# The norms of three seven-product stages: sums by a one-column matrix, rstd to rows by way of DRAM

## The chip, the cores and the metric

The kernel runs on one core of one Trainium2 chip. The metric is the device time of one execution in microseconds (us), as the median of several runs.

## The reference

One inference step of a decoder trunk of two layers, for 1,024 prompt tokens and 64 sample tokens that share their weights (1,088 tokens, model width 1,024). Layer 0 mixes tokens by sparse attention, layer 1 by a chunked gating unit; a SwiGLU follows each.

```python
def rms_norm(x, g):
    xf = x.astype(jnp.float32)
    y = xf * lax.rsqrt(jnp.mean(xf * xf, axis=-1, keepdims=True) + EPS)
    return (y * g.astype(jnp.float32)).astype(x.dtype)

def swiglu(h, w_gu, w_down):
    gate, up = jnp.split(h @ w_gu, 2, axis=-1)
    return (jax.nn.silu(gate) * up) @ w_down

# for each layer i
        xp = xp + mp          # mixer(rms_norm(x)): attention, or the gating unit (h @ w_in, gelu, ...)
        xs = xs + ms
        xp = xp + swiglu(rms_norm(xp, norm_ffn[i]), ffn_w_gu[i], ffn_w_down[i])
        xs = xs + swiglu(rms_norm(xs, norm_ffn[i]), ffn_w_gu[i], ffn_w_down[i])
```

The change concerns three of the norms: those ahead of the two SwiGLUs and the one ahead of the gating unit.

## The kernel before

Activations lie in SBUF with features on the 128 partitions and the 1,088 tokens along a row (`xT`, eight tiles). Each float32 operand is split in a high and a low part (ScalarE writes the high part, `high...`; VectorE subtracts for the low part, `low`, `w_low`), and TensorE multiplies high by high, high by low and low by high.

The three stages of the change are `ffn_stage`, run twice (`ffn0`, `ffn1`), and `gate_stage` (`sgin`). Each multiplies the activations by weights in sets, and each set is made of seven block products (a Strassen scheme with `PRODUCTS = 7`), named p = 0 to 6 here: `B11, T1, T2, B21, T3, B22, T4`. A product is 24 matmuls with 272 columns into one of four pairs of PSUM banks. `ffn_stage` has 22 sets, `gate_stage` eight. The weights of set n + 1 are summed, split and made ready by VectorE and ScalarE while TensorE works on set n, and so are the results of set n combined: `make_u2`, `make_u4`, `make_g0` (the gate's left half, times `rows`), `make_c22` and so on. Product 6 of a set writes the banks that `make_c22` reads, so it waits for it: `FREE_NOW = {3: t_ready, 5: u2_ready, 6: c22_ready}`.

The gain of the norm is put on the activations ahead of the products; the factor 1/rms of each token (`rstd`) is put on the results afterwards, by a multiplication with `rows`, a [128, 1088] tile that holds the token's rstd on every partition. It is made during set 0, in this order: ScalarE squares the last tile into `rows`, VectorE adds the squares of the others; TensorE sums over partitions with the squares as the stationary operand (`column_sums_wide`, bank 6) between products 1 and 2; VectorE and ScalarE make rstd from the sums, which are a [128, 9] tile (`Rstd`: mean, square root, reciprocal and a Newton step); TensorE spreads rstd to all partitions by nine matmuls against the identity (`SPREAD`), between products 2 and 3; ScalarE copies the result to `rows`.

The order of every engine's work is written out by hand; nothing is scheduled by a planner. Waits are on semaphores. SyncE issues nearly all DMAs; a set's weights are loaded (`load_set`) once the low parts of the set before are written. The attention part has a `search_stage` with norms of its own, which are made in the other way: a matrix with one column of ones (`pick`) is stationary, the squares move, the sums land as 8 rows of 136 tokens (`PairRstd`), and rstd goes through DRAM (`r_kept`) to rows.

## Time and profile before

| | |
|---|---|
| median of 3 runs | 2520.27 us (2519.26 to 2523.59) |
| the profiled execution's own time | 2533.14 us |
| its span in the trace | 2531.4 us |
| TensorE (PE) busy | 2444.0 us, 97% of the span |
| VectorE (DVE) busy | 1827.9 us, 72% |
| ScalarE (ACT) busy | 1130.0 us, 45% |
| GpSimd (POOL) busy | 108.3 us, 4% |
| mean granted TensorE clock | 0.987 of full speed |

The profiled execution is one of its own and took 0.5% longer than the median; its trace is read for durations and waits. Busy shares are means over stages that differ. The `ffn0` stage begins at 778 us of the span, `sgin` at 1488 us, `ffn1` at 1804 us; set 0 takes the first 26 us or so of each.

### The profile page before, as it was taken

To read this page: it belongs to the slowest core of one execution; us is meant where nothing else is said; L and a number is where in the kernel's file an instruction comes from. 1 tells how busy PE (TensorE), PEld (TensorE's weight loads), DVE (VectorE), ACT (ScalarE), POOL (GpSimd) and SP (SyncE) were. 2 spreads that over 40 slices of the span, in tenths; PEclk is the share of its full clock that TensorE was granted. 3 is DMA by queue.
4 is the path that set the end of the run, shared out by engine and by line. 5 is a ranking of instruction groups with operands and counts; after the bars stand their busy time and mean duration, and the time that the engine had idled before them with its cause. 6 is when DMAs were issued, how large, how long until landed. Compare 5 with 4: busy or idle time off the path is not lost. (4 is left out here: it accounts for less than half of the span.)

```text
span 2531.4 us, 49311 instructions
## 1 busy us (share of the span) xinstructions
PE 2444.0 (97%) x18922; PEld 2332.5 (92%) x18953; DVE 1827.9 (72%) x3377; ACT 1130.0 (45%) x1928; POOL 108.3 (4%) x140
## 2 busy tenths in 40 slices
PE   8999898899999999999999999989999999999998
PEld 7899865577899999999999999989999999999998
DVE  6668867777558888886685686764798888768642
ACT  5567677686534433333222353553443434322221
POOL 1310132200000000000000000000000000000000
PEclk9899999999999999999999999999999999999999
DMA  6312499820022343433694423234143434449522
GB/s 213 88 51 80 145 332 361 329 84 1 21 100 70 139 147 138 147 138 124 241 321 150 134 73 113 68 94 168 56 139 138 148 138 151 140 177 351 193 91 84
DMA packets 279016, 371.91 MB, mean 147 GB/s; under 512 B 20747, under 2 KB 219651, under 8 KB 270662
## 3 DMA queue, kind: packets, MB, share of 16 engines
q1 hardware_dynamic: 266998, 294.23, 34.3%
q0 software_dynamic: 11776, 75.50, 8.1%
q8 instruction: 101, 1.65, 0.3%
q14 instruction: 61, 0.50, 0.1%
q10 hardware_dynamic: 80, 0.02, 0.0%
HBM read 271.07 MB, written 98.63 MB: 146 GB/s over the span
## 5 line engine op out<-in xcount | busy, mean ns | idle before, releaser
L1554 PE MATMUL ffn_acc<-trunk_x_ahead,trunk_w_hi 128*128 128x272 f32 x2464 | 466.5, 289 | 2.7 <-PEq L87 2.7
L1554 PE MATMUL ffn_acc<-ffn_x_later,ffn_w_hi_more 128*128 128x272 f32 x2112 | 397.1, 287 | 1.5 <-DVE trunk_xT L1203 1.4
L1554 PEld LDWEIGHTS ffn_acc<-trunk_x_ahead,trunk_w_hi 128*128 128x128 f32 x2464 | 385.3, 188 | 3.3 <-issue 3.3
L1554 PE MATMUL ffn_acc<-trunk_x_ahead,trunk_w_lo 128*128 128x272 f32 x1232 | 352.9, 286 | 0.0
L1554 PEld LDWEIGHTS ffn_acc<-ffn_x_later,ffn_w_hi_more 128*128 128x128 f32 x2112 | 330.9, 188 | 2.3 <-issue 2.3
L1554 PE MATMUL ffn_acc<-ffn_x_later,ffn_w_lo_more 128*128 128x272 f32 x1056 | 304.1, 288 | 0.0
L1554 PEld LDWEIGHTS ffn_acc<-trunk_x_ahead,trunk_w_lo 128*128 128x128 f32 x1232 | 232.5, 189 | 0.0
L1554 PEld LDWEIGHTS ffn_acc<-ffn_x_later,ffn_w_lo_more 128*128 128x128 f32 x1056 | 198.8, 188 | 0.0
L1445 DVE TENSOR_TENSOR trunk_xT<-ffn_acc,trunk_xT 128x544 f32<-128x544 f32 x168 | 121.4, 723 | 92.9 <-PE ffn_acc L1610 91.0
L1610 PE MATMUL ffn_acc<-trunk_x_ahead,trunk_w_hi 128*128 128x272 f32 x896 | 170.8, 289 | 0.0
L945 ACT ACTIVATE ffn_w_hi_more<-trunk_w_raw 128x512 fp32r<-128x512 f32 x132 | 83.3, 631 | 156.2 <-PE ffn_acc L1554 153.5
L945 ACT ACTIVATE trunk_w_hi<-ffn_w_sum 128x512 fp32r<-128x512 f32 x88 | 55.6, 632 | 210.2 <-DVE ffn_w_sum L1184 125.4
L1610 PE MATMUL ffn_acc<-ffn_x_later,ffn_w_hi_more 128*128 128x272 f32 x768 | 145.8, 287 | 0.1
L1634 PE MATMUL ffn_acc<-trunk_x_ahead,trunk_w_hi 128*128 128x364 f32 (+1 forms) x576 | 142.1, 328 | 0.0
L1610 PEld LDWEIGHTS ffn_acc<-trunk_x_ahead,trunk_w_hi 128*128 128x128 f32 x896 | 140.1, 188 | 0.4 <-issue 0.4
L1610 PE MATMUL ffn_acc<-trunk_x_ahead,trunk_w_lo 128*128 128x272 f32 x448 | 128.3, 286 | 0.0
L3321 PE MATMUL search_acc<-attxm_x_pairs,attxm_w_hi 128*128 128x364 f32 (+1 forms) x480 | 121.4, 334 | 1.9 <-PEq L87 1.9
L1610 PEld LDWEIGHTS ffn_acc<-ffn_x_later,ffn_w_hi_more 128*128 128x128 f32 x768 | 120.2, 188 | 0.7 <-issue 0.3
L1032 ACT ACTIVATE trunk_xT<-trunk_xT 128x544 fp32r<-128x544 f32 x112 | 71.7, 654 | 91.5 <-DVE trunk_xT L1264 48.8
L1610 PE MATMUL ffn_acc<-ffn_x_later,ffn_w_lo_more 128*128 128x272 f32 x384 | 110.5, 288 | 0.0
L1203 DVE TENSOR_TENSOR trunk_xT<-ffn_acc,ffn_u 128x544 f32<-128x544 f32 x88 | 63.5, 722 | 59.2 <-PE ffn_acc L1554 59.2
L1634 PEld LDWEIGHTS ffn_acc<-trunk_x_ahead,trunk_w_hi 128*128 128x128 f32 x576 | 101.8, 188 | 0.0
(523 smaller groups left out, 5994.6 us busy)
## 6 DMA issues: line engine op xcount, KB each, us to landing
o_kept<-trunk_xT SPq DMA_DIRECT2D x96, 544.0 KB, 4.4
trunk_w_raw<-in_ffn_w_gu SPq DMA_DIRECT2D x88, 512.0 KB, 4.0
trunk_x_ahead<-o_kept SPq DMA_DIRECT2D x56, 544.0 KB, 6.7
ffn_x_later<-o_kept SPq DMA_DIRECT2D x56, 544.0 KB, 7.3
x_saved<-trunk_xT SPq DMA_DIRECT2D x24, 544.0 KB, 2.7
trunk_xT<-x_saved SPq DMA_DIRECT2D x24, 544.0 KB, 6.6
o_kept<-trunk_xT SPq DMA_DIRECT2D x32, 272.0 KB, 4.9
trunk_w_raw<-in_sg_w_in SPq DMA_DIRECT2D x16, 512.0 KB, 4.0
```

The lines of the kernel that those rows point to most:

```text
L945: nc.scalar.activation(w_parts(i)[0], source, ACT.Copy).then_inc(w_hi_ready, 1)
L1032: nc.scalar.activation(stage_hi[STAGE_OF[i][0]], raw_block[i], ACT.Copy).then_inc(kept_hi, 1)
L1203: nc.vector.tensor_tensor(two(out), pair(b), two(a), ALU.add).then_inc(done, 1)
L1445: nc.vector.tensor_tensor(two(out), pair(bank_of(z, n)), two(out), ALU.add).then_inc(d_added, 1)
L1554: last = nc.tensor.matmul(bank(2 * PAIR[p] + c)[:, 0:QC], w[:, k * P:(k + 1) * P], x(p, k)[:, c * QC:(c + 1) * QC], start=FRESH[p] and k = ...
L1610: last = nc.tensor.matmul(bank(2 * bank_of(z, n) + c)[:, 0:QC], w[:, k * P:(k + 1) * P], x(i, at)[:, c * QC:(c + 1) * QC], start=n in (0, ...
L1634: last = nc.tensor.matmul(bank(NC3 * (q % 2) + c)[:, 0:w], part[:, q % 2, k * P:(k + 1) * P], x[:, a:a + w], start=(k == 0 and j == 0), st ...
L3321: last = nc.tensor.matmul(banks[NC3 * (m % 2) + c][:, 0:w], part[:, k * P:(k + 1) * P], x_parts[x][:, k, a:a + w], start=(k == 0 and j == ...
```

## The change

Three things are done in `ffn_stage` and `gate_stage`. The sums over partitions are made as in `search_stage`: a [128, 32] window on a matrix with one column of ones is stationary and 136 tokens of squares move, in eight matmuls that fill four groups of 32 PSUM partitions (`row_sums`). rstd is then made on [128, 136] tiles (those of `Rstd` lie in `g0`, in the gate stage in `v_sq`). The nine spreading matmuls and ScalarE's three copies are gone; ScalarE issues four DMAs that store rstd's rows to DRAM (`s_kept`) and, four activations later, one that loads it to all 128 partitions of `rows`. On VectorE, `make_g0(0)` moves from the middle of the `low(T4, ...)` steps to behind `sum_1(1)`, and in the gate stage `make_c11(0)` and `norm_c22(0)` move there too. `pick` becomes one tile for the whole trunk, filled in the first stage.

```diff
-def column_sums_wide(nc, out, squares, ones):
-    for t in range(NTT):
-        a = min(t * P, TOK - P)
-        last = nc.tensor.matmul(out[:, t:t + SUM_W], squares[:, a:a + P], ones[:, 0:SUM_W], start=True, stop=True)
+def row_sums(nc, out, squares, pick):
+    for f in range(2):
+        for c in range(4):
+            a = (2 * c + f) * PIECE
+            last = nc.tensor.matmul(out[32 * c:32 * c + 32, 0:PIECE], pick[:, 3 - f:35 - f], squares[:, a:a + PIECE],
+                                    start=f == 0, stop=f == 1, skip_group_check=True)
     return last
...
-        R = Rstd(S, bank(6)[:, 0:NTT], NTT, D)
+        R = Rstd(S, bank(6)[:, 0:PIECE], PIECE, D, tiles=g0)
...
-            for i, (t0, t1, b, at) in enumerate(SPREAD):
-                act.wait_ge(spread, i + 1)
-                x0, x1 = t0 * P, min(t1 * P, TOK)
-                nc.scalar.activation(rows[:, x0:x1], bank(b)[:, at:at + x1 - x0], ACT.Copy).then_inc(rows_ready, 1)
+            act.wait_ge(R.link, R.READY)
+            for c in range(4):
+                act.dma_start(s_kept[c], R.r[32 * c:32 * c + 2, :]).then_inc(rows_kept, 16)
             for k in range(KH):
                 high(B22, k)
+            act.wait_ge(rows_kept, 64)
+            act.dma_start(rows[:, :], s_kept.rearrange("c f n -> (c f n)").unsqueeze(0).to_broadcast([P, TOK])).then_inc(rows_ready, 16)
             for k in range(KH):
                 high(T4, k)
...
             make_u2(0)
-            dve.wait_ge(rows_ready, 3)
             make_u4(0)
             for k in range(KH):
                 low(B22, k)
-            low(T4, 0)
-            low(T4, 1)
-            make_g0(0)
-            low(T4, 2)
-            low(T4, 3)
+            for k in range(KH):
+                low(T4, k)
             make_c22(0)
             low_1(1)
             sum_1(1)
+            dve.wait_ge(rows_ready, 16)
+            make_g0(0)
             w_low(1, 2, A_S1, E[:, :])
...
-            column_sums_wide(nc, bank(6), rows, g["ones"]).then_inc(summed, 1)
+            row_sums(nc, bank(6), rows, g["pick"]).then_inc(summed, 1)
             product(0, 2, True)
-            pe.wait_ge(R.link, R.READY)
-            for t0, t1, b, at in SPREAD:
-                for tt in range(t0, t1):
-                    skip = tt * P - min(tt * P, TOK - P)
-                    last = nc.tensor.matmul(bank(b)[:, at + (tt - t0) * P:at + (tt - t0 + 1) * P - skip],
-                                            R.r[:, tt:tt + 1].to_broadcast([P, P]), g["ident"][:, skip:P],
-                                            start=True, stop=True)
-                last.then_inc(spread, 1)
             product(0, 3, True)
-            pe.wait_ge(rows_ready, 3)
+            pe.wait_ge(R.link, 1)
             for p in range(4, PRODUCTS):
                 product(0, p, True)
```

The same edits are made in `gate_stage`, where `norm_c22(0)` follows `make_c11(0)` behind `sum_1(1)`. In the first stage GpSimd sets `pick` to zero and writes its column; in `search_stage` it no longer does.

VectorE in set 0 of `ffn0`, from the low parts of `B22` and `T4` to the first low part of set 1's weights; `ffn_x_later` are the low parts of activations, `trunk_xT<-ffn_acc,ffn_u` is `make_c22`, `ffn_gate` is `g0`. Before:

```order
L1151 TENSOR_TENSOR ffn_x_later<-trunk_xT,ffn_x_later 128x544 x6
L1215 TENSOR_TENSOR ffn_gate_10897<-ffn_acc,ffn_rows 128x544
L1151 TENSOR_TENSOR ffn_x_later<-trunk_xT,ffn_x_later 128x544 x2
L1203 TENSOR_TENSOR trunk_xT<-ffn_acc,ffn_u_10898 128x544
L1176 TENSOR_TENSOR trunk_w_lo<-trunk_w_raw,trunk_w_hi 128x1024
L1184 TENSOR_TENSOR ffn_w_sum<-trunk_w_raw 128x512
L1172 TENSOR_TENSOR trunk_w_lo<-ffn_w_sum,trunk_w_hi 128x512
```

And of the change, the same place:

```order
L1156 TENSOR_TENSOR ffn_x_later<-trunk_xT,ffn_x_later 128x544 x8
L1208 TENSOR_TENSOR trunk_xT<-ffn_acc,ffn_u_10891 128x544
L1181 TENSOR_TENSOR trunk_w_lo<-trunk_w_raw,trunk_w_hi 128x1024
L1189 TENSOR_TENSOR ffn_w_sum<-trunk_w_raw 128x512
L1220 TENSOR_TENSOR ffn_gate_10890<-ffn_acc,ffn_rows 128x544
L1177 TENSOR_TENSOR trunk_w_lo<-ffn_w_sum,trunk_w_hi 128x512
```

The multiplication by `rows` now stands behind `make_c22`, `low_1(1)` and `sum_1(1)`.

ScalarE at the same time: `L1010` are the copies to `rows`, `L939` the high parts of `B22` and `T4`. Before:

```order
L945 ACTIVATE ffn_w_hi_more<-trunk_w_raw 128x512
L939 ACTIVATE ffn_x_later<-trunk_xT 128x544
L1010 ACTIVATE ffn_rows<-ffn_acc 128x512 x2
L1010 ACTIVATE ffn_rows<-ffn_acc 128x64
L939 ACTIVATE ffn_x_later<-trunk_xT 128x544 x8
L956 ACTIVATE trunk_w_hi<-trunk_w_raw 128x1024
```

And of the change:

```order
L949 ACTIVATE ffn_w_hi_more<-trunk_w_raw 128x512
L943 ACTIVATE ffn_x_later<-trunk_xT 128x544
L1013 DMA s_kept<-ffn_gate_10890 2x136 x4
L943 ACTIVATE ffn_x_later<-trunk_xT 128x544 x4
L1017 DMA ffn_rows<-s_kept 128x1088
L943 ACTIVATE ffn_x_later<-trunk_xT 128x544 x4
L960 ACTIVATE trunk_w_hi<-trunk_w_raw 128x1024
```

Three copies have given way to five DMA issues, the last between the high parts of `B22` and those of `T4`.

VectorE at the end of set 0 in `gate_stage`; `trunk_xT<-sgin_acc,sgin_t_u` is `make_c22`, `trunk_xT<-sgin_acc,sgin_rows` is `make_c11`, `trunk_xT<-trunk_xT,sgin_rows` is `norm_c22`. Before:

```order
L2180 TENSOR_TENSOR trunk_xT<-sgin_acc,sgin_rows 128x544
L2102 TENSOR_TENSOR trunk_x_low<-trunk_xT,trunk_x_low 128x544 x2
L2185 TENSOR_TENSOR trunk_xT<-sgin_acc,sgin_t_u_16348 128x544
L2164 TENSOR_TENSOR trunk_xT<-trunk_xT,sgin_rows 128x544
L2127 TENSOR_TENSOR trunk_w_lo<-trunk_w_raw,trunk_w_hi 128x1024
L2135 TENSOR_TENSOR sgin_w_sum<-trunk_w_raw 128x512
L2123 TENSOR_TENSOR trunk_w_lo<-sgin_w_sum,trunk_w_hi 128x512
```

And of the change:

```order
L2101 TENSOR_TENSOR trunk_x_low<-trunk_xT,trunk_x_low 128x544 x2
L2184 TENSOR_TENSOR trunk_xT<-sgin_acc,sgin_t_u_16331 128x544
L2126 TENSOR_TENSOR trunk_w_lo<-trunk_w_raw,trunk_w_hi 128x1024
L2134 TENSOR_TENSOR sgin_w_sum<-trunk_w_raw 128x512
L2179 TENSOR_TENSOR trunk_xT<-sgin_acc,sgin_rows 128x544
L2163 TENSOR_TENSOR trunk_xT<-trunk_xT,sgin_rows 128x544
L2122 TENSOR_TENSOR trunk_w_lo<-sgin_w_sum,trunk_w_hi 128x512
```

Both multiplications by `rows` now come after `sum_1(1)`, in the order `make_c11`, `norm_c22`.

## Rows read from the trace of the kernel before

**Rows 1.** PE timeline, set 2 of ffn0 and sgin: start, length, ..., [idle, releaser]

```profile
844.42 0.49 PE L1554 MATMUL ffn_acc<-ffn_x_later,ffn_w_hi_more 128*128 128x272 f32 x2 [0.69 <-DVE trunk_xT L1203]
...
1554.45 0.48 PE L2373 MATMUL sgin_acc<-sgin_x_high,sgin_w_hi_more 128*128 128x272 f32 x2 [1.25 <-DVE trunk_xT L2185]
```

**Rows 2.** PE timeline of set 0 in ffn0

```profile
785.22 2.14 PE L191 MATMUL ffn_acc<-trunk_ones,ffn_rows 128*128 128x96 f32 x18
...
790.24 2.12 PE L1569 MATMUL ffn_acc<-trunk_ident,ffn_rstd 128*128 128x128 f32 x18
...
801.46 0.50 PE L1554 MATMUL ffn_acc<-ffn_x_later,ffn_w_hi_more 128*128 128x272 f32 x2
```

**Rows 3.** DVE timeline of set 0 in ffn0

```profile
787.48 0.17 DVE L162 TENSOR_SCALAR ffn_mean<-ffn_acc 128x9 f32<-128x9 f32 x1
...
788.19 0.21 DVE L166 RECIPROCAL ffn_rinv<-ffn_root 128x9 f32<-128x9 f32 x1
...
789.13 0.69 DVE L1172 TENSOR_TENSOR ffn_w_lo_more<-trunk_w_raw,ffn_w_hi_more 128x512 fp32r<-128x512 f32 x1
...
798.74 0.72 DVE L1215 TENSOR_TENSOR ffn_gate<-ffn_acc,ffn_rows 128x544 f32<-128x544 f32 x1
799.38 1.35 DVE L1151 TENSOR_TENSOR ffn_x_later<-trunk_xT,ffn_x_later 128x544 fp32r<-128x544 f32 x2
800.64 0.71 DVE L1203 TENSOR_TENSOR trunk_xT<-ffn_acc,ffn_u 128x544 f32<-128x544 f32 x1
...
802.41 0.68 DVE L1184 TENSOR_TENSOR ffn_w_sum<-trunk_w_raw 128x512 f32<-128x512 f32 x1
803.79 0.69 DVE L1172 TENSOR_TENSOR trunk_w_lo<-ffn_w_sum,trunk_w_hi 128x512 fp32r<-128x512 f32 x1 [0.70 <-ACT trunk_w_hi L945]
```

**Rows 4.** busy time by window, from 788 to 801 us

```profile
788.00:801.00 13.00, 13.00 (x109) 13.00 (x108) 12.77 (x25) 9.76 (x18) 0.00 (x0) 1.00 0.30 82
```

**Rows 5.** ACT timeline of set 0 in ffn0

```profile
791.54 1.39 ACT L1010 ACTIVATE ffn_rows<-ffn_acc 128x512 f32<-128x512 f32 x3
792.82 4.49 ACT L939 ACTIVATE ffn_x_later<-trunk_xT 128x544 fp32r<-128x544 f32 x8
```

**Rows 6.** PE timeline of the search stage, one head's sums

```profile
197.07 0.67 PE L3275 MATMUL search_small<-att_proj,search_pick 128*32 128x136 f32 x16
```

**Rows 7.** DVE timeline of the search stage, mean and rstd of a pair

```profile
185.02 0.30 DVE L3127 TENSOR_SCALAR search_head_mean<-search_small 128x136 f32<-128x136 f32 x1
...
189.71 0.99 DVE L3137 RECIPROCAL search_head_rinv<-search_head_root 128x136 f32<-128x136 f32 x1
...
191.88 0.15 DVE L2529 TENSOR_TENSOR search_late_over<-search_late_count,search_late_limit 128x2 f32<-128x2 f32 x1
```

**Rows 8.** SP queue of the search stage, and landing times of its row loads

```profile
192.00 1.32 SPq L3216 DMA_DIRECT2D r_kept<-search_head_rstd  x4
194.23 0.94 SPq L3222 DMA_DIRECT2D search_row_buf<-r_kept  x2
...
DMA to landing us min/median/max: 4.0/4.6/5.5
```

**Rows 9.** DVE and PE timeline of set 0 in sgin

```profile
1509.19 0.72 DVE L2185 TENSOR_TENSOR trunk_xT<-sgin_acc,sgin_t_u 128x544 f32<-128x544 f32 x1
...
1510.59 1.22 DVE L2127 TENSOR_TENSOR trunk_w_lo<-trunk_w_raw,trunk_w_hi 128x1024 fp32r<-128x1024 f32 x1
...
1510.88 0.41 PE L2373 MATMUL sgin_acc<-sgin_x_high,sgin_w_hi_more 128*128 128x272 f32 x2
```

**Rows 10.** DMA issues by size, KB each, median us to landing

```profile
trunk_xT<-x_kept SPq DMA_DIRECT2D x8, 544.0 KB, 9.0
```

**Rows 11.** busy time and granted clock (PEclk) by window: one long idle, one short

```profile
17.70:21.60 3.90, 0.06 (x2) 0.02 (x1) 2.38 (x4) 3.13 (x5) 0.12 (x1) 0.79 0.10 1
21.60:26.60 5.00, 5.00 (x17) 3.85 (x18) 5.00 (x5) 5.00 (x5) 0.00 (x0) 0.50 0.22 2
53.50:58.50 5.00, 3.23 (x20) 3.22 (x20) 4.23 (x8) 3.60 (x8) 0.00 (x0) 1.00 0.00 1
```

More of the change, by code:

```diff
@@ L138, with __init__ @@
 class Rstd:
-    def __init__(self, S, sums, columns, width, name="", like=None, out=None):
+    def __init__(self, S, sums, columns, width, name="", like=None, out=None, tiles=None):
         self.sums, self.width = sums, width
-        if like is None:
+        if tiles is not None:
+            self.mean, self.root, self.y, self.a = (tiles[:, columns * i:columns * (i + 1)] for i in range(4))
+            self.r = self.root
+        elif like is None:
             self.mean, self.root, self.y, self.a, self.r = (S.sb(name + n, [P, columns]) for n in
```

83 lines of the change are left out of this document (34 added, 49 removed).

## The prediction

> **What bounds the kernel now.** I read the page first: TensorE is busy for 97% of the span, so work taken from it looks like time won. But that share is an average, and the change acts in the first 26 us of three stages, so I read next who is waited for there. In set 2 of `ffn0` TensorE stands still for 0.69 us, and in set 2 of `sgin` for 1.25 us, each time for `make_c22`, which frees the banks of product 6 [rows 1]; `ffn1` has the same wait as `ffn0`. The timeline of VectorE shows why: from 788 to 801 us it works for 12.77 of 13.00 us [rows 4] (the columns there are the window, its length, the busy time of TensorE, its weight loads, VectorE, ScalarE and GpSimd, the granted clock, the DMA share and GB/s). Its rows of set 0 follow one another with no idle in brackets, up to the one that waits 0.70 us for a high part [rows 3]. In `ffn0` it stays that full until set 2. So the clock of these stages, from the norm to product 6 of set 2, is VectorE's list of work and not TensorE's; behind that TensorE sets the pace. The reader is to see that two engines are nearly full here, and that the one which ends the wait in set 2 is VectorE.
>
> **The change part by part.**
>
> TensorE. The sums are 18 matmul records of 2.14 us, the spreading 18 of 2.12 us [rows 2]. In the search stage the new form of the sums is 16 records of 0.67 us [rows 6]. By lengths, up to 2.14 + 2.12 - 0.67 = 3.6 us a stage are taken off TensorE. What they are worth is decided by the next point.
>
> VectorE. rstd is made on 136 columns in place of 9. From the reciprocal to the next piece of work it is 789.13 - 788.19 = 0.94 us now [rows 3], and 191.88 - 189.71 = 2.17 us for the same five operations on 136 columns [rows 7]: 1.23 us more. The first step grows from 0.17 to 0.30 us [rows 3, 7], 0.13 more. Together VectorE is 1.36 us later from there on. Ahead of `make_c22(0)`, `make_g0(0)` is taken out, 799.38 - 798.74 = 0.64 us [rows 3]. So `make_c22(0)` begins at 800.64 + 1.36 - 0.64 = 801.36, 0.72 us late. Behind it `make_g0(0)` falls between `sum_1(1)` at 802.41 and the low part at 803.79, where VectorE waits 0.70 us for ScalarE [rows 3]; 0.64 us go in there for nothing. That cover holds as long as the gap stays. From here the 0.72 us are carried through to `make_c22(2)`, and TensorE's wait of rows 1 ends 0.72 us later: it does not matter that TensorE comes 3 us early to product 6 of set 0.
>
> The same in `sgin`, up to the end of `make_c22(0)`: +1.36 - 0.64. There `norm_c22(0)` also moves. `make_c22` and `norm_c22` take 1510.59 - 1509.19 = 1.40 us now [rows 9]; `make_c22` alone takes 0.64, so 0.76 come off. But two multiplications go into the gap of 0.70 us, where one fits: from `sum_1(1)` to the low part it is 1.38 us now and would be 0.60 + 0.64 + 0.65 = 1.89, 0.51 more. The sum is 1.36 - 0.64 - 0.76 + 0.51 = +0.47 us, carried to set 2 through the loads that VectorE's low parts release. Product 6 of set 0 has 0.97 us of slack there (`make_c22` ends at 1509.91, the product begins at 1510.88 [rows 9]), so that alone does not decide.
>
> The Trainium skill says in "VectorE: DVE Perf Modes", section "The TRN2 errata", that such an operation pays a fixed cost and then about a cycle per element at 0.96 GHz. By it the six operations would grow by 127 elements each, 0.79 us in all as an estimate, and the whole change would come to about +0.2 us. The rows say otherwise of one of the six: the reciprocal goes from 0.21 to 0.99 us [rows 3, 7], 6.1 ns a column, so I sum by the rows.
>
> ScalarE. Now the three copies begin at 791.54 and the high parts of `B22` at 792.82 [rows 5], 1.28 us. A DMA issue by ScalarE does not appear in this stretch. Its cost lies between nothing and that of SyncE's, 1.32 us for four [rows 8]; I take the latter. With VectorE 1.36 us late, ScalarE comes to the stores at 792.90, to the high parts of `B22` at 794.2 and, at 0.56 us for each of four, to the load of `rows` at 796.5. Stored rows can be read 194.23 - 192.00 = 2.23 us after the first issue [rows 8], at 795.1: no wait. The high parts of `T4` then begin at 797.0; VectorE wants the first at 798.8, finished, so 1.3 us are to spare.
>
> The load of `rows`. In the search stage it lands 4.0 to 5.5 us after its issue, 4.6 in the middle [rows 8]: at 800.5 to 802.0. `make_g0(0)` wants it at 802.41 + 0.72 + 0.60 = 803.7. To spare are 1.7 to 3.2 us, and in `sgin`, where two low parts of 0.64 us fewer stand ahead, about 0.4 to 1.9. I take 4.6, and so no wait.
>
> Outside the three stages: one more fill by GpSimd in the first stage, and five fewer in the search stage. Nothing there waits for them: nothing.
>
> **Sum:** 0.72 + 0.47 + 0.72 = +1.9 us. On the profiled execution, 2533.14 becomes 2535.0 us. That execution is 0.5% slower than the median; the terms are short pieces and do not grow with it, so I add them to the median: 2520.3 + 1.9 = 2522.2 us. With every term of VectorE at nothing but `make_g0` gone (0.64 off in each stage, the lower bound), it would be 2518.4 us. A measurement of this kernel can tell about 0.2%, 5.0 us, from no change.
>
> **The rivals.**
>
> TensorE's saving comes through. Then 3 x 3.6 = 10.8 us go, and the time is 2509.5 us. For it speaks the busy share of 97%. Against it: the waits for `make_c22` in set 2 [rows 1], and no idle time in VectorE that could be given up. It would need VectorE to be some 3 us quicker than its rows. Parts of it (ScalarE or the loads running more freely than I think) would give 2511 to 2515. Chance 0.05, and 0.05 for the parts.
>
> The rows come late. In these stages two weight loads of 512 KB are issued shortly ahead, which the search stage has not. The slowest median for a load of this size, 544 KB, is 9.0 us [rows 10]. Then `make_g0(0)` waits 9.0 - 7.2 = 1.8 us in both `ffn` stages and 9.0 - 5.9 = 3.1 us in `sgin`, each carried to set 2 like the rest: 6.7 us more, 2528.9 us. The point from which it decides is a landing of about 8 us in all three stages (0.8 + 0.8 + 2.1 = 3.7 us). Against it: the search stage never needed more than 5.5 us. Chance 0.07.
>
> The clock falls. TensorE now has to wait in set 0. Product 5 cannot begin before the first low part of `B22`, which is six slots of 0.64 us ahead of 798.74, plus 0.72 us, plus the 1.36 us: 797.0. A product takes about 5.02 - 2.14 = 2.9 us [rows 2], and product 6 waits for `make_c22` until 802.1, some 2.2 us. After 3.9 us with hardly any matmul the granted clock was 0.50, the 1.2 GHz level, for the next 5 us; after an idle of 1.77 us (5.00 - 3.23) it stayed at 1.00, the 2.4 GHz level [rows 11]. My 2.2 us lie nearer the second. If the clock fell in all three stages, 5 us at half speed cost 2.5 us each: 1.9 + 7.5, 2529.7 us. Chance 0.05. The Trainium skill, "TensorE: Matmul & The Clock Gate", section "HAM oscillation", warns of this: waits between bursts of matmuls send the array back to half clock. No row of this trace has an idle of the length in question, so the page neither settles it nor moves the chance.
>
> My own case, that nothing measurable changes, is robust against the price of rstd: from nothing (2518.4 us) up to twice the 1.36 us (4.1 us more, 2526.3 us) only the top end leaves 0.2%.
>
> **How the numbers follow.** My case has 0.76, and by itself 2518.4 (the lower bound) to 2525 us (the rows late by 1 us or so in each stage). The faster cases have 0.10; rows late, clock and whatever else costs over 5 us have 0.14. The range for 8 in 10 reaches into both, 2515.5 to 2527.5 us. Faster by over 0.2%: 0.10, within: 0.76, slower: 0.14.
>
> **What would show it right or wrong.** In the changed kernel's trace: the sums in 0.6 to 0.7 us; VectorE's reciprocal near 1.0 us and `make_c22(0)` of `ffn0` 0.7 us later behind the start of the stage; TensorE idle ahead of product 6 of set 0, for about 2 us; the waits of rows 1 still there, and about as long; `make_g0(0)` with no wait for a DMA; clock 1.00 in all three stages. I am wrong if the waits in set 2 are gone, if `make_g0(0)` waits for the rows, or if the stages show a clock under 1.

## The result and the profile after

The changed kernel takes 2528.04 us (median of 11 runs, 2525.58 to 2530.41) where the kernel before takes 2522.67 us beside it (11 runs): a ratio of 1.0023, 95% interval 1.0015 to 1.0031, so 5.8 us slower (3.8 to 7.8; the two medians differ by 5.4). The forecast was +1.9 us and "no difference that can be measured", added to a median of 2520.27 us to give 2522.2 us. The kernel before reads 2.4 us more in these 11 runs than there; that much of the distance to 2528.04 us is not the change. The profiled execution took 2525.6 us.

The page of the changed kernel, span and busy shares:

```profile
span 2523.8 us, 49193 instructions
PE 2431.1 (96%) x18862; PEld 2320.4 (92%) x18893; DVE 1832.2 (73%) x3377; ACT 1126.8 (45%) x1919; POOL 107.8 (4%) x137
```

TensorE is busy 12.9 us less than before, as the change meant it. To see why that bought nothing I laid each stage on its own start (TensorE's first matmul there): `ffn0` begins at 764.32, `sgin` at 1477.13, `sgout` at 1694.87, `ffn1` at 1793.90, and the store stage at 2505.46 us; times written with a plus count from such a start. `ffn0` takes 712.81 us (709.67 before), `ffn1` 711.56 (708.30), `sgin` 217.74 (216.48); the attention stages ahead of `ffn0` vary by up to 18 us over the executions of this study, so spans are not compared.

VectorE in set 0 of `ffn0`, changed kernel (start, duration of the group, line, output and inputs):

```profile
772.69 0.29 DVE L166 TENSOR_SCALAR ffn_gate<-ffn_acc 128x136 f32<-128x136 f32 x1
773.53 0.99 DVE L170 RECIPROCAL ffn_gate<-ffn_gate 128x136 f32<-128x136 f32 x1
...
775.49 0.30 DVE L178 TENSOR_TENSOR ffn_gate<-ffn_gate 128x136 f32<-128x136 f32 x1
775.71 0.69 DVE L1177 TENSOR_TENSOR ffn_w_lo_more<-trunk_w_raw,ffn_w_hi_more 128x512 fp32r<-128x512 f32 x1
...
786.53 0.71 DVE L1208 TENSOR_TENSOR trunk_xT<-ffn_acc,ffn_u 128x544 f32<-128x544 f32 x1
...
788.30 0.68 DVE L1189 TENSOR_TENSOR ffn_w_sum<-trunk_w_raw 128x512 f32<-128x512 f32 x1
788.90 0.71 DVE L1220 TENSOR_TENSOR ffn_gate<-ffn_acc,ffn_rows 128x544 f32<-128x544 f32 x1
789.68 0.69 DVE L1177 TENSOR_TENSOR trunk_w_lo<-ffn_w_sum,trunk_w_hi 128x512 fp32r<-128x512 f32 x1
```

rstd takes 775.71 - 773.53 = 2.18 us, `make_c22(0)` starts at +22.21 (786.53), 0.69 us later than before [rows 3], and `make_g0(0)` at 788.90 has no wait and fills the gap. That is the forecast for VectorE, row for row. TensorE beside it (the bracket is idle time before the row, and its releaser):

```profile
770.41 0.67 PE L196 MATMUL ffn_acc<-ffn_rows,trunk_pick 128*32 128x136 f32 x16
...
777.78 0.49 PE L1557 MATMUL ffn_acc<-ffn_x_later,ffn_w_hi_more 128*128 128x272 f32 x2 [0.47 <-DVE ffn_x_later L1156]
...
782.32 0.49 PE L1557 MATMUL ffn_acc<-ffn_x_later,ffn_w_hi_more 128*128 128x272 f32 x2 [1.10 <-DVE ffn_x_later L1156]
...
787.35 0.59 PE L1557 MATMUL ffn_acc<-ffn_x_later,ffn_w_hi_more 128*128 128x272 f32 x2 [1.81 <-issue]
...
1861.07 0.49 PE L1557 MATMUL ffn_acc<-ffn_x_later,ffn_w_hi_more 128*128 128x272 f32 x2 [0.32 <-DVE trunk_xT L1208]
```

The sums take 0.67 us in place of 2.14 [rows 2], and the time won comes back as three waits of set 0, ahead of products 4, 5 and 6: 3.38 us in all. In set 2 the wait for `make_c22` is gone in `ffn0` and down to 0.32 us in `ffn1` (1861.07); before it was 0.69 [rows 1]. Something had made TensorE as late as VectorE. The windows of the same stretch say what (columns as in [rows 4]; the granted clock is the third number from the end):

```profile
779.32:785.32 6.00, 4.90 (x38) 4.55 (x36) 5.97 (x11) 3.41 (x7) 0.00 (x0) 1.00 0.87 231
785.32:788.32 3.00, 1.19 (x7) 1.00 (x6) 3.00 (x6) 1.06 (x1) 0.00 (x0) 0.88 0.33 78
788.32:791.32 3.00, 3.00 (x16) 3.00 (x15) 2.94 (x6) 0.63 (x1) 0.00 (x0) 0.55 0.00 0
791.32:794.32 3.00, 3.00 (x26) 3.00 (x25) 2.27 (x5) 2.68 (x4) 0.00 (x0) 1.00 0.00 0
...
1496.13:1501.13 5.00, 3.19 (x26) 3.00 (x25) 5.00 (x8) 0.78 (x2) 0.00 (x0) 1.00 0.34 93
...
1817.90:1820.90 3.00, 3.00 (x17) 3.00 (x17) 2.94 (x6) 0.63 (x1) 0.00 (x0) 0.58 0.00 0
```

Behind the 1.81 us the clock falls to near 0.50, the 1.2 GHz level, for about 3 us, in `ffn0` and in `ffn1`: 16 matmul records in 3 us where 26 is normal. In `sgin` (1496 to 1501), with a wait of 1.81 us too, it stays at 1.00. Set 1 of `ffn0` starts at +27.64, 2.22 us later than before (+25.42), not 0.7.

There is a second difference, far from the change. A steady set of the `ffn` stages should take the same time in both kernels. VectorE waits for product 5 once a set (`make_g1`), which makes a good stopwatch; here are the rows of one early and one late set, 17 sets apart, in `ffn0` of the kernel before:

```profile
865.71 0.72 DVE L1203 TENSOR_TENSOR trunk_xT<-ffn_acc,ffn_u 128x544 f32<-128x544 f32 x1 [1.57 <-PE ffn_acc L1554]
...
1222.70 0.72 DVE L1203 TENSOR_TENSOR trunk_xT<-ffn_acc,ffn_u 128x544 f32<-128x544 f32 x1 [1.48 <-PE ffn_acc L1554]
```

and of the changed kernel:

```profile
852.25 0.72 DVE L1208 TENSOR_TENSOR trunk_xT<-ffn_acc,ffn_u 128x544 f32<-128x544 f32 x1 [1.57 <-PE ffn_acc L1557]
...
1209.70 0.72 DVE L1208 TENSOR_TENSOR trunk_xT<-ffn_acc,ffn_u 128x544 f32<-128x544 f32 x1 [1.55 <-PE ffn_acc L1557]
```

356.99 us against 357.45: 21.00 us a set against 21.03, with no wait in either. It is 0.13%, but of 1,420 us.

### The profile page after: what moved, and what is told of

The parts are those of the page before. It is cut to its first block and busy times, and to the rows that moved or that the text cites. A ratio compares the mean times of both kernels' runs of the same rounds, so it can differ in the third digit from the quotient of the medians.

```text
span 2523.8 us, 49193 instructions
## 1 busy us (share of the span) xinstructions
PE 2431.1 (96%) x18862; PEld 2320.4 (92%) x18893; DVE 1832.2 (73%) x3377; ACT 1126.8 (45%) x1919; POOL 107.8 (4%) x137
## 3 DMA queue, kind: packets, MB, share of 16 engines
q10 hardware_dynamic: 560, 1.71, 0.2%
```

## The experiments

All kernels were run beside the kernel before; ratios are to those runs. "Sets" is the steady set of `ffn0` / `ffn1`; "at set 3" is that same wait of VectorE in set 3, the fourth, counted from the start of `ffn0` / `ffn1`: it sums up all that went late up to there. "One run" stands where a kernel was run once, so that its time says little.

| kernel | ratio to before | sets, us | at set 3, us |
|---|---|---|---|
| before | 1 | 21.00 / 21.00 | +86.59 / +86.58 |
| changed | 1.0023 [1.0015, 1.0031] | 21.03 / 21.03 | +87.93 / +88.48 |
| e1 before, `pick` allocated | 1.0006 [0.9997, 1.0015] | 21.03 / 21.03 | +86.69 / +86.47 |
| e2 changed, TensorE kept busy | 1.0022 [1.0013, 1.0032] | 21.03 / 21.03 | +87.20 / +87.60 |
| e3 changed, c22(0) early | 1.0018 [1.0009, 1.0027] | 21.03 / 21.03 | +87.99 / +88.37 |
| e4 changed, c22(2) early | 1.0008 [0.9999, 1.0017] | 21.03 / 21.03 | +88.15 / +88.71 |
| e5, e6, e7 before, 64, 96, 128 bytes | one run each (2520.6, 2521.7, 2520.8 us; before 2521.9) | 20.98 / 20.98; 21.08 / 20.92; 20.99 / 20.99 | all +86.55 to +86.88 |
| e8 changed, Newton on GpSimd | 1.0029 [1.0018, 1.0041] | 21.03 / 21.03 | +87.49 / +87.47 |
| e9 changed, 32 bytes more | 0.9998 [0.9986, 1.0009] | 20.91 / 20.91 | +87.59 / +89.48 |
| e10 changed, gaps filled | 1.0022 [1.0010, 1.0033] | 21.03 / 21.03 | +88.78 / +87.93 |
| e11 before, gaps filled | 0.9986 [0.9977, 0.9996] | 21.00 / 21.00 | +85.62 / +85.62 |
| e12 combined | 0.9989 [0.9980, 0.9998] | 20.91 / 20.91 | +87.33 / +86.40 |
| e14 combined, 8 small matmuls | 0.9974 [0.9965, 0.9983] | 20.91 / 20.91 | +86.48 / +86.29 |
| e15 before, gaps filled, address | 0.9969 [0.9956, 0.9981] | 20.91 / 20.91 | +85.35 / +85.34 |
| e13, e16, e17 changed, 8, 1, 3 small matmuls | one run each (2525.0, 2530.9, 2530.8 us; before 2522.1, 2524.9, 2524.9) | 21.03 / 21.03 in all | +87.63 / +88.08; +87.95 / +90.01; +90.02 / +88.40 |

**e1: the address alone.** A tile named `pick` makes everything allocated behind it lie 160 bytes further on; the activations' operands go from SBUF byte 17952 of a partition to 18112. The high and low parts of the weights stay for four of the seven products; those of the other three (`ffn_w_hi_more`, `ffn_w_lo_more`) lie in the same stretch of memory and move along by 160 bytes, as `rows` and `g0` do. So "the address" here and below is that of the whole stretch, and no run moves the activations alone (the expectation of e5, that the weights' parts are in one place in all kernels, holds for those four products only).

```diff
-        g = {"ones": T.sb("ones", [P, P]), "ident": T.sb("ident", [P, P])}
+        g = {"ones": T.sb("ones", [P, P]), "ident": T.sb("ident", [P, P]), "pick": T.sb("pick", [P, 35])}
```

> The kernel before, with one unused [128, 35] tile (`pick`) allocated in the trunk, so that all later SBUF tiles lie 140 bytes or so further on; nothing else changes and nothing is left out. In the two traces at hand a steady set of the ffn stages takes 21.00 us before and 21.03 us after the change. Theory A (the addresses of the operands slow the matmuls a little): the set takes 21.03 us here too, and the kernel is about 1 us slower than before. Theory B (that difference comes from something else, or from the one execution that was profiled): 21.00 us, and a time within 0.5 us of before. What is worth 2.2 us at the start of each ffn stage does not show here by either.

```profile
854.75 0.72 DVE L1203 TENSOR_TENSOR trunk_xT<-ffn_acc,ffn_u 128x544 f32<-128x544 f32 x1 [1.57 <-PE ffn_acc L1554]
...
1212.20 0.72 DVE L1203 TENSOR_TENSOR trunk_xT<-ffn_acc,ffn_u 128x544 f32<-128x544 f32 x1 [1.63 <-PE ffn_acc L1554]
```

These are the same two rows as above, of e1: 357.45 us, the pace of the changed kernel to the hundredth, without a line of the change. `ffn0` takes 711.36 us here and `ffn1` 709.50, 1.7 and 1.2 more than before; of that the sets are 0.46 each, the rest the part of the stage behind them, which multiplies by the down weights (that rest is not as sure as the sets; see below). The total, 1.5 us slower (-0.8 to 3.8), agrees with theory A and by itself does not settle it.

**e2: TensorE kept busy.** (changed kernel)

```diff
+            def keep_busy(count):
+                if count:
+                    pe.wait_ge(u4_ready, 1)
+                for _ in range(count):
+                    nc.tensor.matmul(bank(3)[:, QC:QC + 96], g["ones"][:, :], g["ones"][:, 0:96], start=True, stop=True)
...
             for p in range(4, PRODUCTS):
+                keep_busy({4: 0, 5: 4, 6: 7}[p])
                 product(0, p, True)
```

> The changed kernel, with matmuls on a tile of ones into unused columns of a PSUM bank while TensorE waits in set 0 of both ffn stages: four (about 0.9 us) ahead of product 5 and seven (about 1.7 us) ahead of product 6. Their results are read by nobody. The order and the work of all other engines stay. Theory 1 (the granted clock falls because TensorE stands still ahead of product 6, and this costs 1.5 us a stage that the later stall in set 2 hides only in part): the clock stays at 1.00 through product 6, set 1 begins at +26.2 us of the stage in place of +27.6, and the stages are 0.7 to 1.4 us shorter each; 1.5 to 2.8 us less than the changed kernel in all. Rival 2 (VectorE's list alone explains the loss): the clock may stay up, but set 2 begins its stall as before, and the time is that of the changed kernel within 0.5 us. Rival 3 (the added matmuls stand in the way): up to 0.6 us slower a stage.

The fillers, the wait in set 2, and the stretch in which the clock had fallen:

```profile
782.89 0.35 PE L1567 MATMUL ffn_acc<-trunk_ones 128*128 128x96 f32 x1 [0.38 <-DVE ffn_u L1208]
...
831.74 0.36 PE L1557 MATMUL ffn_acc<-ffn_x_later,ffn_w_hi_more 128*128 128x272 f32 x1 [0.78 <-DVE trunk_xT L1208]
```

```profile
788.63:792.63 4.00, 3.98 (x32) 4.00 (x33) 3.93 (x6) 0.64 (x1) 0.00 (x0) 1.00 0.00 0
```

The clock stays at 1.00 in both stages, the wait of set 2 is back (0.78 us), and set 3 is 0.73 and 0.88 us earlier: what the fall of the clock costs, net of the wait that it hides. What is left over before, 0.61 and 1.02 us, stands against the forecast's 0.72. The total does not show it: 1.0022. `sgin`, which this edit does not touch, took 219.95 us in the profiled run, and 215.0 to 220.0 over all kernels; effects of 1 to 2 us are read in the stages, not in the totals.

**e3: `make_c22(0)` earlier.** (in the three stages)

```diff
+            make_c22(0)
             for k in range(KH):
                 low(T4, k)
-            make_c22(0)
             low_1(1)
```

> The changed kernel with one piece of VectorE's order moved in all three stages: `make_c22(0)` ahead of the four low parts of T4 in place of behind them, so 2.6 us earlier. Nothing is left out. If the wait ahead of product 6 and the fall of the clock behind it are the cause (theory 1), product 6 of ffn begins near +21.1 us of the stage without a wait over 0.4 us, the clock stays at 1.00, the wait moves to the start of set 1 (VectorE's low part and g0 there end at about +25.3), and each ffn stage ends 0.6 to 1.4 us sooner: 1.2 to 3 us less in all. If VectorE's list up to set 2 is all that counts (rival 2), nothing changes in total, since the list is as long as it was.

TensorE's waits in `ffn0`, the new ones:

```profile
788.13 0.49 PE L1557 MATMUL ffn_acc<-trunk_x_ahead,trunk_w_hi 128*128 128x272 f32 x2 [1.05 <-DVE ffn_gate L1220]
...
807.22 0.49 PE L1557 MATMUL ffn_acc<-ffn_x_later,ffn_w_hi_more 128*128 128x272 f32 x2 [0.72 <-DVE trunk_xT L1208]
...
829.37 0.49 PE L1557 MATMUL ffn_acc<-ffn_x_later,ffn_w_hi_more 128*128 128x272 f32 x2 [0.86 <-DVE trunk_xT L1208]
```

The wait ahead of product 6 is gone and the clock stays up, yet set 3 is where it was: TensorE waits at the start of set 1 (for `g0`), in set 1 and in set 2. A wait on an engine whose supplier is full moves when it is pushed. The outcome is that of rival 2, but it is not clean. VectorE waits for a weight load in set 1 of both stages, which in the changed kernel it did for 0.13 and 0.04 us:

```profile
803.15 0.69 DVE L1189 TENSOR_TENSOR ffn_w_sum<-trunk_w_raw 128x512 f32<-128x512 f32 x1 [0.39 <-DMA trunk_w_raw<-in_ffn_w_gu]
...
1833.14 0.69 DVE L1189 TENSOR_TENSOR ffn_w_sum<-trunk_w_raw 128x512 f32<-128x512 f32 x1 [0.81 <-DMA trunk_w_raw<-in_ffn_w_gu]
```

If the 0.39 and 0.81 us had not been lost, set 3 would be at about +87.6 in both stages (an estimate, if they are passed on whole), which is near e2's +87.20 and +87.60. So e3 does not speak against a price of the fallen clock; part of what it won there went to the late load.

**e4: `make_c22(2)` earlier** (`n == 2` in the gate stage likewise).

```diff
             def prepare(n, early=False):
...
                 make_g0(n)
+                if early:
+                    make_c22(n)
                 low_1(n + 1)
                 sum_4(n + 1)
-                make_c22(n)
+                if not early:
+                    make_c22(n)
...
-            prepare(2)
+            prepare(2, True)
```

> The changed kernel with `make_c22` of set 2 ahead of low_1 and sum_4 of the next set (1.85 us earlier in VectorE's list) in all three stages; set 0 as it is. Nothing is left out. It takes the stall of set 2 away that hid part of what set 0 loses. In the changed kernel 0.3 us or so of that stall are left in an ffn stage and 1.3 in sgin. Theory 1: the ffn stages gain 0 to 0.3 us each, sgin 1.0 to 1.3, the clock still falls in set 0 of ffn; 1 to 2 us less in all. Rival 2 (VectorE's list sets the pace to the end of set 2 and would be late anywhere): the stall comes back at another wait of set 2 or 3 and nothing is gained.

`sgin` was the shortest of all, 214.97 us. Theory 1 had it 1.0 to 1.3 us shorter than in the changed kernel; it was 2.8 us, and this stage varies by as much without such an edit. The `ffn` stages held two surprises. TensorE waits 1.80 us ahead of product 6 as in the changed kernel, yet the clock stays at 1.00: whether it falls is not decided by the length of that wait alone. And TensorE then waits in set 1, because VectorE waits for a load there:

```profile
808.05 0.69 DVE L1189 TENSOR_TENSOR ffn_w_sum<-trunk_w_raw 128x512 f32<-128x512 f32 x1 [1.67 <-DMA trunk_w_raw<-in_ffn_w_gu]
```

```profile
812.12 0.36 PE L1560 MATMUL ffn_acc<-ffn_x_later,ffn_w_hi_more 128*128 128x272 f32 x1 [1.52 <-DVE trunk_xT L1208]
```

**e5, e6, e7: other addresses** (kernel before with a `pad` tile; 64 bytes shown).

```diff
-        g = {"ones": T.sb("ones", [P, P]), "ident": T.sb("ident", [P, P])}
+        g = {"ones": T.sb("ones", [P, P]), "ident": T.sb("ident", [P, P]), "pad": T.sb("pad", [P, 16])}
```

> The kernel before with 64 unused bytes a partition allocated in the trunk: the activations' operands begin at an SBUF address of 96 modulo 128 bytes (32 in the kernel before, 64 with `pick`, in the changed kernel too; the weights' high and low parts are at 96 in all). Nothing is left out. Theory A (the address modulo a small power of two sets the pace of the matmuls): a steady set of ffn0 and ffn1 takes a time that goes with this remainder and not with the distance, 21.00 us or less here if 64 is the bad one. Theory C (any tile ahead of the arena slows them): 21.03 us.

> As with 64 bytes, but 96: the operands begin at 0 modulo 128 bytes. Theory A: the set takes 21.00 us or less if a multiple of 128 is good, and 21.03 us if it is whether the address is a multiple of 64 that slows it. Theory C: 21.03 us.

> As with 64 bytes, but 128: the operands begin at 32 modulo 128 bytes, as in the kernel before. Theory A: a set takes 21.00 us as before, and the down part has its length of before (245.1 and 243.7 us from the last gate result to the end of the stage, within 0.3 us). Theory C: 21.03 us and about 1 us more in the down part.

Operands at 18016, 18048 and 18080 give 20.98, 21.08 or 20.92 (`ffn0`, `ffn1`) and 20.99 us a set. So not every shift slows (theory C falls), and the pace does go with the address: over all kernels the 17 sets take 357.00 us in four of four stages at 17952, 357.45 in 20 of 20 at 18112 and 355.41 in eight of eight at 18144, to 0.01 us. But the remainder modulo 128 does not order it: 18144 (e9, below) has the remainder of 18016 and runs at 20.91. And at 18048 (e6) `ffn0` and `ffn1` differed by 0.16 us a set in one execution, so something besides the address plays a part there; what, stays open.

**e8: the Newton step on GpSimd** (in the three stages).

```diff
+def rest_on_pool(R, nc, pool):
+    pool.wait_ge(R.link, 2)
+    nc.gpsimd.tensor_tensor(R.a[:, :], R.y[:, :], R.y[:, :], ALU.mult).then_inc(R.link, 1)
...
+    nc.gpsimd.tensor_tensor(R.r[:, :], R.a[:, :], R.y[:, :], ALU.mult).then_inc(R.link, 1)
...
-            R.rest(nc, dve)
+            dve.wait_ge(R.root_ready, 1)
+            nc.vector.reciprocal(R.y[:, :], R.root[:, :]).then_inc(R.link, 1)
```

> The changed kernel with the four operations of the Newton step of rstd moved from VectorE to GpSimd in the three stages; the reciprocal stays on VectorE, and nothing is left out. It takes 2.17 - 0.99 = 1.18 us from VectorE's list ahead of `make_c22(0)`. Theory 1 (VectorE's list up to product 6 is what the change made longer): `make_c22(0)` of ffn begins at +21.0 us of the stage in place of +22.2, TensorE's waits in set 0 shrink by about 1.1 us together, the clock does not fall, and the last event of the sets comes 1.2 us or more earlier in both ffn stages: 2.5 to 5 us less in all than the changed kernel. Rival (GpSimd is so slow that the rows of rstd come late, or it holds VectorE up at the shared SBUF): the four operations take over 4 us together, `make_g0(0)` then waits for the rows, and the time is that of the changed kernel or more.

GpSimd, and VectorE beside it:

```profile
774.36 0.73 POOL L183 TENSOR_TENSOR ffn_gate<-ffn_gate 128x136 f32<-128x136 f32 x1 [301.92 <-DVE ffn_gate L1353]
775.16 0.80 POOL L185 TENSOR_TENSOR ffn_gate<-ffn_gate 128x136 f32<-128x136 f32 x1
776.05 0.66 POOL L187 TENSOR_SCALAR ffn_gate<-ffn_gate 128x136 f32<-128x136 f32 x1
776.80 0.83 POOL L189 TENSOR_TENSOR ffn_gate<-ffn_gate 128x136 f32<-128x136 f32 x1
```

```profile
774.74 0.89 DVE L1219 TENSOR_TENSOR trunk_w_raw<-trunk_w_raw,ffn_w_sum 128x512 f32<-128x512 f32 x1
775.55 1.00 DVE L1171 TENSOR_TENSOR ffn_x_later<-trunk_xT,ffn_x_later 128x544 fp32r<-128x544 f32 x1
```

The two VectorE rows take 0.68 and 0.72 us without GpSimd. Of the 1.18 us taken from VectorE it won 0.44 (`make_c22(0)` at +21.77), and the clock fell in all three stages, `sgin` included, where TensorE waited 3.79 us ahead of product 6. The Trainium skill tells of such a contention in "GPSIMD Engine Reference", section "Specifications": GpSimd's SBUF interface is shared with VectorE and contends with its instructions that have two SBUF inputs. The trace agrees, 0.89 against 0.68 us for an operation with two inputs in SBUF.

**e9: 32 bytes more** (changed kernel, operands at 18144).

```diff
-        g = {"ones": T.sb("ones", [P, P]), "ident": T.sb("ident", [P, P]), "pick": T.sb("pick", [P, 35])}
+        g = {"ones": T.sb("ones", [P, P]), "ident": T.sb("ident", [P, P]), "pick": T.sb("pick", [P, 35]), "pad": T.sb("pad", [P, 8])}
```

> The changed kernel with 32 more unused bytes behind `pick`, so that the operands begin at 96 modulo 128 bytes, the remainder at which a set took 20.98 us in the kernel before with 64 bytes. Nothing else changes. Theory A (the address makes part of the loss): a set takes 20.98 to 20.99 us in place of 21.03, the 17 sets 0.7 to 0.8 us less, and an ffn stage with its down part 1 to 2 us less, so 2 to 4 us in all; the start of the stages keeps its waits. Theory C (it is something else in the changed kernel): 21.03 us and no change.

20.91 us a set, where 20.98 to 20.99 was expected, 2.0 us less for 17 sets of each stage, and the ratio is 0.9998 in place of 1.0023, with every wait of set 0 still there and a late load in `ffn1` on top. (Before ran at 2529 us beside the kernels e9 to e12 and at 2522 elsewhere; only ratios are compared.)

**e10 and e11: VectorE's gaps filled**, in the changed kernel and in the kernel before. In e11 `sum_3(1)` also goes ahead of `w_low(1, 2)` in set 0, where the kernel before has a gap that `make_g0(0)` fills in the changed one.

```diff
+                sum_3(n + 1)
                 w_low(n + 1, 2, A_S1, E[:, :])
-                sum_3(n + 1)
...
+            make_g1(0)
             w_low(1, 3, A_S2, E[:, :])
-            make_g1(0)
```

> The changed kernel with VectorE's waits of 0.70 us for a high part filled, in the three stages: `sum_3` of the next set ahead of the low part for which VectorE waits (from set 1 on), and in set 0 `make_g1(0)` (`make_c12(0)` in sgin) ahead of `w_low(1, 3)`. The work is the same. Theory 1 (VectorE's list from the norm to product 6 of set 2 is what binds): `make_c22(1)` and `make_c22(2)` come 1.2 to 1.9 us earlier, TensorE no longer waits in set 1 or 2, and the last event of the sets comes 0 to 0.3 us earlier than in the changed kernel (whose stall in set 2 is nearly gone already), in sgin 1.0 to 1.3 us earlier: 1 to 2 us less in all. The rest of the loss, waits and clock in set 0, stays. Rival: the stalls are of loads and not of the list, and nothing changes.

> The same filling of VectorE's gaps in the kernel before (`sum_3` of the next set ahead of the low part, and `make_g1(0)` ahead of `w_low(1, 3)`). It tells whether the stall in set 2 of the kernel before was VectorE's list: if so, the 0.69 and 0.70 us of the ffn stages and the 1.25 us of sgin are gone, 2.6 us less than before in all (0.1%). If the list is not what binds there, no change.

In e11 TensorE has no wait at all between +12 and +90 of either `ffn` stage, set 3 is 0.97 us earlier, and the kernel is 0.14% faster than before: the stall in set 2 [rows 1] was VectorE's list, as the prediction said, and that list had gaps to give. In e10, `ffn0` ran into the late load again (VectorE waits 2.33 us), and nothing was gained.

**e12: combined.** e3, e9 and e10 together, with `make_g0(0)` (`make_c11(0)` in `sgin`) ahead of `low_1(1)`.

```diff
             make_c22(0)
             for k in range(KH):
                 low(T4, k)
+            dve.wait_ge(rows_ready, 16)
+            make_g0(0)
             low_1(1)
             sum_1(1)
```

> The changed kernel with all that the runs so far point to: 32 bytes of alignment, `make_c22(0)` ahead of the low parts of T4, `make_g0(0)` ahead of low_1, and VectorE's gaps filled as in the two other kernels. Nothing is left out. Theory 1: set 1 of ffn begins near +24.8 us (25.4 before, 27.6 in the changed kernel), the clock stays at 1.00, no stall in sets 1 and 2; each ffn stage ends 1.3 to 1.6 us earlier than before, sgin 1.5 us, some 4 us (0.16%) less than before and 9 less than the changed kernel. Rival (VectorE late anyway, a wait for g0 or for the weights' parts in set 1): no better than the kernel before.

Set 1 of `ffn` starts at +24.75, as expected, and the clock stays up, but TensorE waits for `make_c22(1)`, 0.68 us in `ffn1` and 1.71 in `ffn0`, where the load landed late once more (after 5.3 us).

**e13, e14, e16, e17: who makes the load late?** The load of set 2's second weight tile is issued at about +35.6 in the changed kernels and wanted by VectorE at about +40.1. In `before` it landed after 4.1 us, in e4 after 6.1 (issue with size and us to landing):

```profile
trunk_w_raw<-in_ffn_w_gu SPq DMA_DIRECT2D x1, 512.0 KB, 4.1
```

```profile
trunk_w_raw<-in_ffn_w_gu SPq DMA_DIRECT2D x1, 512.0 KB, 6.1
```

Every 10 to 20 us there is one transfer on queue 8, "instruction", of about 1 us, at a different place in each kernel. The edit puts small matmuls ahead of product 3 (8, 1 or 3 of them), so that TensorE is further on in its instructions at a given time:

```diff
             product(0, 2, True)
+            for _ in range(8):
+                nc.tensor.matmul(bank(7)[:, QC:QC + 8], g["ones"][:, :], g["ones"][:, 0:8], start=True, stop=True)
```

> The changed kernel with eight small matmuls (8 columns of ones into unused columns of a PSUM bank, read by nobody) behind product 2 of set 0 of both ffn stages. In the 22 ffn stages looked at so far, the load of set 2's second weight tile (issued at +35.6) landed after 4.0 to 4.5 us where the transfer of the instruction queue (one packet on queue 8) fell before +36 or after the landing, and after 4.8 to 6.7 us where it fell between +36.6 and +40.2; in the changed kernel it falls at +40.7 and +40.9, and the 22 records that the kernel with fillers has more moved it to +35.7. Theory F (TensorE's place in its instruction stream decides when the packet comes, and the packet in the middle of the load makes it late): the packet moves 1 to 3 us forward, to +37.5 to +39.9, the load lands after 5 to 6.7 us, VectorE waits for it 0.5 to 2.3 us, and where the clock did not fall TensorE waits for `make_c22(1)`. Rival G (the late landings go with TensorE's speed, not with the packet): late only in a stage in which the clock stayed at 1.00, wherever the packet is.

> The combined kernel with the same eight small matmuls. There the packet fell at +35.8 and +35.9, just behind the load's issue at +35.69, and the load landed after 5.3 and 4.1 us. Theory F: the packet moves to +33 to +34.5, both loads land after 4.0 to 4.5 us, VectorE does not wait for a load, the wait for `make_c22(1)` is 0.7 us or less in both stages, and the kernel is 0 to 1 us faster than the combined one, 0.998 to 0.999 of before. Rival G: no change against the combined kernel.

> The changed kernel with one small matmul behind product 2 (eight moved the instruction packet from +40.7 to +35.8 and +35.6, not into the load). Theory F: the packet moves by a tenth of what eight moved it or less, to +39.9 to +40.6 where the clock falls and about 1.4 us earlier where it does not; the load of set 2 lands after 5 to 6.7 us where the packet comes before +40.2, after 4.0 to 4.5 where it comes later. Rival G is already against one stage (clock 1.00 and a landing after 3.9 us); a stage with the packet in the load and a landing under 4.6 us would speak against F.

> The same with three small matmuls. Theory F: the packet comes at +38 to +40.2 and the load of set 2 lands after 5 to 6.7 us in both stages, whether the clock falls or not. VectorE then waits for it 0.5 to 2.3 us. Against F: a packet at +36.6 to +40.0 and a landing under 4.6 us.

Eight moved the packet further than expected, to +35.8 and +35.7, out of the load instead of into it; the loads landed after 3.9 and 5.0 us. In `ffn0`, the punctual one, the clock had stayed at 1.00, and in `ffn1` it had fallen, so rival G falls. Three put the packet at +39.3 (`ffn0`) and +36.3 (`ffn1`, earlier than expected), one at +41.3 and +39.9. `ffn0` of e17:

```profile
trunk_w_raw<-in_ffn_w_gu SPq DMA_DIRECT2D x1, 512.0 KB, 6.6
```

```profile
806.01 0.69 DVE L1189 TENSOR_TENSOR ffn_w_sum<-trunk_w_raw 128x512 f32<-128x512 f32 x1 [2.24 <-DMA trunk_w_raw<-in_ffn_w_gu]
```

```profile
810.08 0.57 PE L1557 MATMUL ffn_acc<-ffn_x_later,ffn_w_hi_more 128*128 128x272 f32 x1 [2.31 <-DVE trunk_xT L1208]
```

Behind that 2.31 us wait, in set 1, the clock of this stage fell for 3.4 us.

Over the 38 `ffn` stages of all kernels: with the packet at +38.5 to +40.2 and the load under way, the landing took 6.1 to 6.7 us in six of six; with the packet 0.5 to 1.1 us behind the issue 4.8 to 5.3 in three of three; in the other 29 it took 3.9 to 5.3, all but three of them 4.5 or less. The placings alone leave a doubt, since a late load is more likely to be under way when the packet comes. The packets themselves settle most of it. The weight load is made of packets of 512 bytes; their number in a window is the count under 2 KB less the count under 512 B. In `ffn1` of e9 the instruction packet runs from +39.84 to +40.80 (1840.10 to 1841.06). The windows from 1839.26 to 1839.84, from 1840.10 to 1841.06 and from 1841.06 to 1841.96:

```profile
DMA packets 124, 0.24 MB, mean 408 GB/s; under 512 B 7, under 2 KB 78, under 8 KB 124
...
DMA packets 147, 0.37 MB, mean 389 GB/s; under 512 B 19, under 2 KB 20, under 8 KB 146
...
DMA packets 176, 0.31 MB, mean 346 GB/s; under 512 B 20, under 2 KB 38, under 8 KB 176
```

71 packets of the load, then one, then 18: while the instruction packet runs, the last packets of the load stand still and all other traffic goes on. So it is in the six late stages: in five the longest pause of the load is 0.80 to 1.02 us and ends within 0.02 us of the instruction packet's end, and in the sixth (`ffn0` of e4, packet at +38.6) a pause of 0.21 us ends so. That 1 us is the packet's doing. The rest is not explained: behind the pause the last packets are slow (27 to 85 ns each; 27 in the changed kernel, whose load is punctual), and in `ffn0` of e10 the load was some 0.7 us behind a punctual one before the packet came.

In e14 theory F had the packet at +33 to +34.5; it came at +35.9 and +35.1. The two loads landed after 4.4 and 4.3 us and set 3 comes 0.85 us sooner in `ffn0`, where e12's load had been late, and 0.11 us in `ffn1`, where it had not. But e12 had its packet at +35.9 in `ffn0` too, so the packet's place does not explain why its load took 5.3 us there and e14's 4.4. The ratio went from 0.9989 to 0.9974; the intervals overlap.

**e15: the kernel before, gaps filled, operands at 18144** (on top of the edits of e11).

```diff
-        g = {"ones": T.sb("ones", [P, P]), "ident": T.sb("ident", [P, P])}
+        g = {"ones": T.sb("ones", [P, P]), "ident": T.sb("ident", [P, P]), "pad": T.sb("pad", [P, 48])}
...
-        touched = S.sb("touched", [P, 1])
+        touched = g["pad"][:, 0:1]
```

> The kernel before with VectorE's gaps filled and with 192 unused bytes a partition, so that the operands begin at the same address as in the aligned and the combined kernels (18144). It has no part of the change. Theory A: a set takes 20.91 us in place of 21.00, 17 sets of each ffn stage 1.6 us less, and the kernel is 3 to 6 us faster than with the gaps filled alone: 0.996 to 0.9975 of before. Then it is faster than the combined kernel, and the change itself is worth nothing or less. If the pace of 20.91 belongs to the changed kernel: 21.00 us a set, 0.9986 of before.

```profile
854.19 0.72 DVE L1203 TENSOR_TENSOR trunk_xT<-ffn_acc,ffn_u 128x544 f32<-128x544 f32 x1 [1.57 <-PE ffn_acc L1554]
...
1209.61 0.72 DVE L1203 TENSOR_TENSOR trunk_xT<-ffn_acc,ffn_u 128x544 f32<-128x544 f32 x1 [1.63 <-PE ffn_acc L1554]
```

355.42 us for 17 sets, and 0.9969 of before: the fastest kernel of the study, with nothing of the change in it. e14, with the change and every repair, reaches 0.9974. The intervals overlap, so no gain from the change itself can be told.

## Why the prediction was wrong

**What held.** What bounds the start of these stages is VectorE's list (e11 shows it, and e3 shows the waits move). It was not as full as "stays that full until set 2" had it: from 801 to 824 us of the kernel before VectorE works 19.89 of 23.00 us, and the gaps of 0.70 us there are what e11 filled. The price of rstd on 136 columns: 2.18 us measured, 2.17 forecast. `make_c22(0)` late by 0.69 us, 0.72 forecast. The load of the rows landed after 4.5 us, 4.6 forecast, and nothing waited for it. TensorE's saving did not come through. With the clock held up (e2), the stages are 0.6 and 1.0 us late at set 3, against 0.72. The Trainium skill's rule in "VectorE: DVE Perf Modes", section "The TRN2 errata", about a cycle per element, had the six operations grow by 0.79 us, an estimate; they grew by 1.36, most of it in the reciprocal. Two of the prediction's own signs of being wrong came true: the wait in set 2 is gone in `ffn0`, and two stages show a clock under 1.

**The step that failed first: "behind that TensorE sets the pace", taken as the same pace.** The prediction listed `pick` as one more tile and priced it at nothing, since nothing waited for its fill. What it costs is where it pushes the operands. The sets alone cost 0.9 us in the two stages, the same in all ten kernels at this address. By the stages' whole lengths in e1, 1.7 and 1.2 us, it is 2.9 us; but the other 2.0 us lie behind set 20, and that part varies at one address: at 18112 it took 265.8 to 267.5 us in `ffn0` (269.5 in e17) and 265.5 to 266.8 in `ffn1`, against 266.1 and 266.3, and 264.7 and 265.1, in the two kernels at 17952. So the address cost 0.9 us, the part that repeats, and up to 2.9. That the pace goes with it is shown by e1, and that such a shift can move the total by e9 (0.9998 at 18144, 1.0023 at 18112); for 17952 against 18112 the total of e1 (-0.8 to 3.8 us) does not tell.

**The step that failed second: the clock, "My 2.2 us lie nearer the second", chance 0.05.** The wait was 1.81 us, shorter than I had it and within a few hundredths of the idle that had kept 1.00 [rows 11], and the clock fell twice in this execution. I looked at that wait alone; there are 0.47 and 1.10 us of waits within 10 us ahead of it, which I had worked out for product 5 and not put beside it. Whether they matter is not shown: in e4, with all three waits, the clock never fell, and in `ffn1` of e13 it fell with 0.22 us ahead of the 1.81. Of all waits of 1.79 to 1.81 us in set 0 (23 in eight kernels and one in `sgin` of e2) 10 of 24 had a fall. So a chance of 0.05 was too low, and no row could have told which stages it would be. Its price was off the other way: not 2.5 us a stage but 0.7 to 0.9 (e2), since set 2 had a wait to swallow the rest. The Trainium skill, "TensorE: Matmul & The Clock Gate", section "HAM oscillation", had warned of waits between bursts of matmuls; the trace now agrees, with 0.55 behind 1.81 us, in these 10 of 24 cases.

**A third, smaller one: the load of set 2.** In variants of the changed kernel the load of set 2's weights came 6.1 to 6.7 us after its issue in six stages, none of which had a fallen clock in set 0 (1.5 to 2.3 us of TensorE's time). The profiled execution of the changed kernel has none of it; how many of its others do is not known. Its slack was near nothing before too (4.1 and 4.3 us of landing, 4.4 to spare); the prediction never asked for it, though it carried its 0.72 us "through" it.

The sum: 1.9 (forecast) + 0.9 to 2.9 (address) + 1.6 (clock) = 4.4 to 6.4 us, against 5.8 measured (3.8 to 7.8). It adds up terms read in one execution of each kernel; the totals do not confirm the clock's share (e2 1.0022, changed 1.0023). The +0.47 us of `sgin` could not be tested: that stage varied by 5 us from kernel to kernel, and what moves it is open. Not tested either is whether the change costs something in the stages ahead of `ffn0`, where `pick` is now filled once and tiles have moved too; they vary by more than the whole effect. Open too are the rule behind the addresses, and what decides whether the clock falls behind equal waits.
